# Moving the sum of squares behind the fourth projection job of a head loop, one Trainium2 core

## What is computed

```python
proj = h @ w_in
q_x, f_x, i_x, g_x = jnp.split(proj, [HK, 2 * HK, 2 * HK + HV], axis=-1)
f = lb + (1.0 - lb) * jax.nn.sigmoid(f_x)
q, k, v = heads(silu(q_x)), heads(1.0 - f), heads(i_x)
b = jnp.cumsum(log_f, axis=3)                     # inside chunks of 32 tokens
a = jnp.where(causal, einsum(q * exp(b - b_ref), k * exp(b_ref - b)), 0.0)
o_intra = a @ v
state = dec * state + k_dec^T v                   # one state per chunk
o = o_intra + q_dec @ state
o = rms_norm(o, o_norm) * silu(g_x)               # norm over the 128 features of a head
return o @ w_o
```

## Time and profile before

| | |
|---|---|
| median of 3 runs | 1909.19 us (1907.77 to 1910.06) |
| the profiled execution, own time | 1907.2 us |
| its span in the trace | 1905.2 us |
| mean granted TensorE clock | 0.945 |
| HGRN2 head loop with its first and last calls | about 1215 to 1467 us of the span |
| one turn of the loop | 31.3 us |

### The profile page before, as it was taken

How to read it: one execution, slowest core, us unless ns; L and a number is a source line. 1 busy time by engine, 2 the same in 40 slices (tenths; PEclk the granted TensorE clock), 3 DMA queues, 4 the chain that set the end, 5 groups by cost and what they waited for, 6 DMA issues and landing times.

```text
span 1905.2 us, 29877 instructions
## 1 busy us (share of the span) xinstructions
PE 1700.1 (89%) x10588; PEld 1373.1 (72%) x10588; DVE 870.4 (46%) x1467; ACT 716.2 (38%) x1129; POOL 636.7 (33%) x385
## 2 busy tenths in 40 slices
PE   4999868778678999899999998699997899999997
PEld 4777737756455676887888887578786787888885
DVE  4644476655566543552212125666665443212125
ACT  1332333322343443452323234566564351323232
POOL 4344400003331112453444445223231544444441
PEclk8999969998788999899999998799999999999998
DMA  9423200001111112223333332122221323333331
GB/s 319 126 85 91 71 7 3 3 2 58 44 39 30 35 36 67 78 78 88 100 88 99 98 93 63 40 66 72 66 66 42 90 68 89 96 91 99 100 93 63
DMA packets 250852, 140.08 MB, mean 74 GB/s; under 512 B 10089, under 2 KB 242624, under 8 KB 250768
## 3 DMA queue, kind: packets, MB, share of 16 engines
q1 hardware_dynamic: 249072, 135.03, 24.2%
q10 hardware_dynamic: 688, 2.23, 0.3%
q0 software_dynamic: 1008, 1.66, 0.3%
HBM read 136.80 MB, written 2.10 MB: 73 GB/s over the span
## 4 chain that ended last, share of the span: by engine, by line
issue 42%; PE 33%; POOL 10%; DVE 9%; DVEq 4%; ACT 1%; POOLq 1%; ACTq 0%
PE bank L659 24%; POOL w_low L505 9%; PE bank L803 2%; PE bank L914 2%; DVE bank L1740 1%; DVEq L1747 1%; DVEq L2110 1%; DVE sum_sq L1740 1%; DVE sum_sq L359 1%; DVE mix_out L1740 1%; PE bank L817 1%; PE bank L1016 1%; POOL param_rows L486 0%; DVE kk_norm L1740 0%; DVEq L2045 0%
## 5 line engine op out<-in xcount | busy, mean ns | idle before, releaser
L505 POOL TENSOR_TENSOR w_low<-w_raw,w_high 128x1024 fp32r<-128x1024 f32 (+1 forms) x236 | 523.2, 2217 | 1144.8 <-ACT w_high L1271 1144.8
L659 PE MATMUL bank<-act_high,w_high 128*128 128x512 f32 x1000 | 399.0, 399 | 16.4 <-POOL w_low L505 14.2
L659 PE MATMUL bank<-act_high,w_low 128*128 128x512 f32 x1000 | 391.3, 391 | 0.0
L659 PE MATMUL bank<-act_low,w_high 128*128 128x512 f32 x1000 | 391.1, 391 | 0.0
L1271 ACT ACTIVATE w_high<-w_raw 128x1024 fp32r<-128x1024 f32 (+1 forms) x236 | 229.4, 973 | 297.7 <-PE bank L659 276.2
L659 PEld LDWEIGHTS bank<-act_high,w_high 128*128 128x128 f32 x1000 | 188.4, 188 | 64.8 <-issue 10.2
L659 PEld LDWEIGHTS bank<-act_high,w_low 128*128 128x128 f32 x1000 | 188.4, 188 | 41.0
L659 PEld LDWEIGHTS bank<-act_low,w_high 128*128 128x128 f32 x1000 | 188.6, 189 | 39.6 <-issue 2.0
L659 PE MATMUL bank<-hid_high,w_high 128*128 128x512 f32 x488 | 191.9, 393 | 4.5 <-DVE mix_out L2303 3.8
L659 PE MATMUL bank<-hid_high,w_low 128*128 128x512 f32 x488 | 191.3, 392 | 0.0
L659 PE MATMUL bank<-hid_low,w_high 128*128 128x512 f32 x488 | 191.2, 392 | 0.0
(11 more groups left out here) (486 smaller groups left out, 2888.0 us busy)
## 6 DMA issues: line engine op xcount, KB each, us to landing
w_raw<-in_mlp_w SPq DMA_DIRECT2D x128, 512.0 KB, 4.0
w_raw<-in_hgrn_w_in SPq DMA_DIRECT2D x32, 512.0 KB, 4.0
w_raw<-in_w_in SPq DMA_DIRECT2D x29, 512.0 KB, 4.0
w_ada_piece<-in_w_ada SPq DMA_DIRECT2D x6, 2048.0 KB, 13.7
w_raw<-in_w_out SPq DMA_DIRECT2D x8, 512.0 KB, 3.8
w_raw<-in_mla_w_o SPq DMA_DIRECT2D x8, 512.0 KB, 3.8
w_raw<-in_hgrn_w_o SPq DMA_DIRECT2D x8, 512.0 KB, 3.8
w_raw<-in_mla_w_in SPq DMA_DIRECT2D x6, 512.0 KB, 4.0
```

The lines of the kernel that those rows point to most:

```text
L505: gp.tensor_tensor(WL[:, c0 % 2, 0:kt, 0:m], WR[:, c0 % 2, 0:kt, 0:m], WH[:, c0 % 2, 0:kt, 0:m].bitcast(F32), ALU.subtract).then_inc(w_lo, 1)
L659: mm = pe.matmul(PB[s][0:m, :], w[:, s, k, 0:m], a[:, k0 + k, :], start=(k == 0 and w is WH and a is hi), stop=(k == kt - 1 and w is WL))
```

## The change

In the turns that have both a head `n` and a head `o`, PE issues the sum of squares after job G0+3 instead of before it. It goes to bank 5 instead of bank 7, in all calls, so the wait for `g_sd` ahead of the transposes is gone. ACT reads the square root's input from bank 5. In the last call, `hgrn(None, 7)`, the place of the sum stays as it was. No instruction with work is added or removed; one PE wait in each of the seven turns of the loop is removed. No DMA is touched.

```diff
                 else:
                     part(W0 + 1, (free["go"], 2), "hgrn_o", 0, 2, HH, HL)
-                if o is not None:
-                    pe.wait_ge(g_sq, o + 1)
-                    pe.matmul(PB[7][:, :], ONES[:, :], OSQ[:, :], start=True, stop=True).then_inc(g_ss, 1)
+                if o is not None and n is None:
+                    square_sum(o)
                 if n is None:
                     part(W0 + 1, (free["go"], 2), "hgrn_o", 2, 4, HH, HL)
                 if n is not None:
                     if o is not None:
                         job(G0 + 3, n * 4, free["g"], n * 4 + 4)
-                        pe.wait_ge(g_sd, o + 1)
+                        square_sum(o)
                     pe.wait_ge(free["g"], n * 4 + 5)
                     for t in range(TT):
                         mm = pe.transpose(PB[7][:, t * P:(t + 1) * P], VF[:, t * P:(t + 1) * P], IDENT[:, :])
                     mm.then_inc(g_vt, 1)
+
+            def square_sum(o):
+
+                pe.wait_ge(g_sq, o + 1)
+                pe.matmul(PB[5][:, :], ONES[:, :], OSQ[:, :], start=True, stop=True).then_inc(g_ss, 1)
...
                 if o is not None:
                     act.wait_ge(g_ss, o + 1)
-                    act.activation(OSD[:, :], PB[7][:, :], ACT.Sqrt, scale=1.0 / P, bias=CST[:, 3:4])\
+                    act.activation(OSD[:, :], PB[5][:, :], ACT.Sqrt, scale=1.0 / P, bias=CST[:, 3:4])\
                         .then_inc(g_sd, 1)
```

## The result

| | before | after |
|---|---|---|
| median | 1908.99 us (1898.85 to 1910.06, 5 runs) | 1940.29 us (1939.02 to 1942.27, 5 runs) |
| span of the profiled execution | 1905.2 us | 1937.6 us |
| mean granted clock | 0.945 | 0.939 |

The ratio is 1.0174 (95% interval 1.0154 to 1.0195): the changed kernel is slower by some 33 us (by the two medians, 31 us). The direction and most of the mechanism were forecast; the size was not: 33 us stand against a forecast of 24. By the ratio the time is 1942, just outside the range that ended at 1941; the median of 1940.29 alone would lie just inside it.

What follows compares the result with a forecast made beforehand. PE was taken as the bound, busy 1700.1 of 1905.2 us, with a chain between ACT and DVE almost without slack. Late chain 19.9 plus clock 4.2 gave +24.1, 1933.3 us; range 1927 to 1941 (8 in 10).

Steps and rivals of the forecast that it cites:

- Removed: the wait for the squares: PE ahead of the sum of squares: job G0+3 fills the wait for ACT's squares, gaining 1.16 us per turn there.
- Moved: the sum, square root late by 2.91 us: Sum starts after job G0+3, at 1315.27; ACT's square root at 1316.42 instead of 1313.51, its table load staying hidden.
- The rival that priced it: ACT's table load for the square root waits for the sum: 1.28 us more per turn, +9.0, 1942; chance 0.04.
- Bank 5: nothing: Sum in bank 5 instead of 7: same matmul and ACT read, no effect unless the turn order changed.
- What PE sees: Waits of 3.1 us for keys and 0.9 us for weights; turn longer by 2.83 us, 19.9 us in all.
- The clock: Head loop: granted clock falls in nearly every turn after the new waits, 0.6 us each, 4.2 us in all.
- the "end" of 1.6 us: Upper end of the clock's cost per turn, with the slow spell wholly in G0+1; 11.2 us over seven turns.
- the rule of the recurring wait: Skill's rule for the head loop: a wait recurring each turn lets the clock fall each time, so matmuls start cold.
- The sum: Whole kernel: 19.9 + 4.2 = +24.1 us, from a median of 1909.2 to 1933.3 us.
- the full price of the clock: Rival: the slow spell lies on G0+1 each turn, 19.9 + 11.2 = +31, 1940; chance 0.07.
- The rival that was faster: Late chain on ACT and DVE is hidden, the 1.16 us per turn won: 8.1 us less, 1901; chance 0.04.
- the slack was 0.13 us: Between `w_low` of G0+1 ready at 1325.72 and PE's start of that job at 1325.85; the prediction turned on it.

Runs made afterwards that it cites:

- experiment 5: Changed kernel with the sum of squares behind 9 of the 24 matmuls of job G0+3: 1908.24 us, ratio 0.9994 to the kernel before.
- experiment 1: Kernel before with only the sum's bank changed to 5 and the wait for `g_sd` removed, sum in its old place: 1910.11 us, ratio 1.001.
- experiment 2: Changed kernel with filler matmuls in both new PE waits, 12 ahead of the keys' wait, 3 behind the increments: 1935.31 us; repeated once, 1923.48 us.
- experiment 3: Changed kernel with only the 3 filler matmuls behind the increments, the first wait left empty: 1931.03 us, ratio 1.0114 to the kernel before.
- experiment 4: Changed kernel with the sum of squares behind 15 of the 24 matmuls of job G0+3: 1919.67 us, ratio 1.0065 to the kernel before.
- experiment 9: Changed kernel, sum behind 9 matmuls of G0+3, next G0+1's high weights made after DVE's product, ahead of the gate's SiLU: 1907.91 us, ratio 1.0003.
- experiment 10: As experiment 9, with DVE's low part of a head's output made behind the next turn's masked scores: 1906.37 us, ratio 0.9982.
- experiment 8: Changed kernel with 13 filler matmuls ahead of the wait for the keys and 4 between the state increments: 1949.2 us, ratio 1.0212.

## Why the prediction was right in its direction and wrong in its size

- *Removed: the wait for the squares.* Right in place and size. That the 1.16 us are worth nothing even where the chain is not late is shown by experiment 5.
- *Moved: the sum, square root late by 2.91 us.* In the first turn DVE waits 3.88 us for the square root instead of 1.08, so 2.80 us late. That the table load does not wait for the sum held: in the second turn it stands at 1284.13, the sum at 1288.29. The rival that priced it is out, though its 1942 is the number that came.
- *Bank 5: nothing.* Right (experiment 1).
- *What PE sees.* Two waits of 3.1 and 0.9 us forecast, 3.13 and 0.77 measured; a turn longer by 2.83 us forecast, by 2.78 with the clock held up (experiment 2). Of the 19.9 us of this term, 19.4 are found: from the first reciprocal to the last, 225.9 us with fillers against 209.2 before, and 2.8 us ahead of the first. One wait came elsewhere: in the last call PE waits 4.98 us for DVE ahead of a piece of the output projection (0.89 before), and then not for the keys.
- *The clock: the step that failed.* "I take 0.6 us per turn, somewhat under the middle", 4.2 us in all, with 11.2 as the far end. Measured are 1.97 us per turn in the mean (36.10 against 34.13) and 1.0 us in the last call: 238.7 us from the first reciprocal to the last against 225.9, so 12.9 us. That the clock falls in nearly every turn was right; its price was mis-sized, by two steps. The slow stretch was taken from one row, 3.2 us long; in five of the seven distances it lasts about twice as long, and so the "end" of 1.6 us was no end (turns up to 2.7 us over 34.1). The trace before had such a long stretch behind a PE wait of 2.13 us (columns as in the earlier trace rows):

```profile
1174.90:1181.60 6.70, 6.01 (x27) 5.93 (x27) 1.39 (x5) 0.59 (x2) 0.30 (x1) 0.50 0.29 82
```

And I let it fall partly into the waits. In the six turns it began between 0.5 us ahead of the increments and 1.7 us behind their start, at most 0.8 us of it lay in a wait, and in the long ones about half of G0+1 ran in it. By the rule of the recurring wait in the Trainium skill ("TensorE: Matmul & The Clock Gate", section "HAM oscillation — how this bites in real kernels") each turn's matmuls start cold. The trace agrees in that each of the seven distances has a slow stretch; experiments 3 and 4 show turns without one, at the same first wait and at shorter ones.

- *The sum.* 19.4 + 12.9 = 32.3 us, against 32.4 between the spans. The rival "the full price of the clock" had the right mechanism, with 11.2 us, and a chance of 0.07; that the range reached almost to the measured time is owed to it.
- *The rival that was faster* fell as argued: the slack was 0.13 us, and experiment 5 indicates that it is not slack at all but the closing of a ring.

## What to carry to other kernels

An idle microsecond on the busiest engine is not free to take: first measure the slack at the far end of what the moved instruction releases, here 0.13 us at the low weights, and move the other steps of that ring with it. Price the clock from several slow stretches and take the longest as the end of the range; a new wait that recurs in each turn can cost much through the clock beside what it costs itself, here 12.9 us beside 19.4. Before a step is moved into an engine's idle time, look at what it sets off on another engine, here POOL, and at what DVE does in that moment.

## What the runs showed of the hardware

- DVE instructions with two SBUF operands take longer beside POOL's weight subtraction: the scan 1.23 us alone and 2.82 beside it, the scaling 0.75 and 2.77, the product with the gate 0.69 and 2.63. In the kernel before and in experiments 5, 9 and 10 the scan started 0.6 to 1.5 us behind POOL's instruction and ended 1.07 to 1.09 us after it in every turn. The state updates, which read one operand from PSUM, do not: they run 0.43 us apart beside it and without it.
- Three 32-row increments and one 128-row filler in alternation take 0.43 us each, where the same work in a row took 0.22 to 0.23 us (experiment 8).
- A PE wait of 3.13 us was followed by the lower clock in two turns and not in four of the same execution (experiment 3), and waits of 1.0 and 0.8 us in two turns of six (experiment 4).
